# Tables of a diagonal state space built in slices during an expert layer, norms on 128 columns, and a fused bias and maximum in two attentions

## What is computed

```
def rmsnorm(x, w):
    y = xf * lax.rsqrt(jnp.mean(xf * xf, axis=-1, keepdims=True) + EPS)
    return (y * w.astype(jnp.float32)).astype(x.dtype)

# first block, layer: h = modulate(rmsnorm(x, norm1_w), shift1, scale1); mixer; x = x + gate1 * mix
#                     h2 = modulate(rmsnorm(x, norm2_w), shift2, scale2); x = x + gate2 * hier_moe(h2)
# chunk_attention:
scores = jnp.einsum('bclhd,bcshd->bchls', q, k_band) * (ATT_HEAD_DIM ** -0.5)
scores = scores + bias[None, None]
p = jax.nn.softmax(scores, axis=-1)

# second block: rms_norm; gmlp and fox_attention; later s5_mixer, feed-forward, gate
# fox_attention (q and k normalised, c the running sum of the log gates):
s = jnp.einsum('bqhd,bkhd->bhqk', qi, k) * scale
s = s + ci.transpose(0, 2, 1)[..., None] - ck[:, :, None, :]
s = jnp.where(kpos[None, :] <= pi[:, None], s, NEG_INF)

# s5_mixer, from a_re, a_im, log_dt, b_re, b_im alone, so from weights:
mag = jnp.exp(lr * dt)
ab_re, ab_im = mag * jnp.cos(li * dt), mag * jnp.sin(li * dt)
bb_re = cr[..., None] * br - ci[..., None] * bi
bb_im = cr[..., None] * bi + ci[..., None] * br
```

## Time and profile before

| what | value |
|---|---|
| median of 3 runs | 2632.39 us (2631.26 to 2634.85) |
| the profiled execution | 2631.74 us, span 2630.0 us |
| mean granted TensorE clock of that execution | 0.944 of full speed |
| PE busy | 2366.2 us (90%) |
| DVE busy | 1558.4 us (59%) |
| ACT busy | 700.7 us (27%) |
| POOL busy | 1484.7 us (56%) |
| DMA | 374.40 MB, 142 GB/s on average |

### The profile page before, as it was taken

One profiled execution on the slowest core, in us unless ns is written; L12 is line 12 of the kernel. 1 busy time (PEld: TensorE's weight loads), 2 busy tenths in 40 slices (PEclk: granted clock), 3 DMA queues, 4 the chain that ended last, 5 costly groups with the idle time before them and its releaser, 6 DMA issues.

```text
span 2630.0 us, 33090 instructions
## 1 busy us (share of the span) xinstructions
PE 2366.2 (90%) x12200; PEld 1806.6 (69%) x12200; DVE 1558.4 (59%) x1986; ACT 700.7 (27%) x1170; POOL 1484.7 (56%) x1272
## 2 busy tenths in 40 slices
PE   4988989959999998896798799999987899999998
PEld 2764755537777776553585588888866788888887
DVE  6879832166878765224897666662249926666223
ACT  2113212223434422122223232220025613222011
POOL 4830345455554552553672166667779657666774
PEclk7977989979999997998897999999998999999999
DMA  8845879533323234994331133332330223333231
GB/s 318 255 162 206 293 285 360 190 125 105 102 91 112 93 112 178 393 357 163 84 116 60 49 96 96 96 96 93 114 97 25 57 64 96 96 96 96 88 112 64
DMA packets 316737, 374.40 MB, mean 142 GB/s; under 512 B 52250, under 2 KB 259886, under 8 KB 316502
## 3 DMA queue, kind: packets, MB, share of 16 engines
q1 hardware_dynamic: 253840, 313.82, 35.6%
q0 software_dynamic: 28352, 31.04, 3.6%
q10 hardware_dynamic: 34438, 28.08, 3.5%
HBM read 410.20 MB, written 39.68 MB: 171 GB/s over the span
## 4 chain that ended last, share of the span: by engine, by line
PE 29%; issue 24%; POOL 23%; DVE 11%; DMA 10%; ACT 1%; POOLq 0%; ACTq 0%; SPq 0%; DVEq 0%
POOL WL L853 15%; PE PAIR L545 6%; POOL WH L849 6%; PE PAIR L546 6%; PE PAIR L547 6%; DMA XG<-htok_scratch,GATHER_I 4%; PE BANK L1823 4%; DMA ADA_A<-in_ada_w 2%; PE BANK L2259 1%; PE PAIR L1847 1%; PE PAIR L1809 1%; DVE ADA_SUM L652 1%; DMA PAIR_W<-y_scratch 1%; POOL EXTRA_W L2007 1%; DMA RAW<-in_ffn_w_up 1%
## 5 line engine op out<-in xcount | busy, mean ns | idle before, releaser
L853 POOL TENSOR_TENSOR WL<-RAW,WH 128x512 fp32r<-128x512 f32 x584 | 819.0, 1432 | 12.2
L545 PE MATMUL PAIR<-HH,WH 128*128 128x512 f32 x1792 | 710.0, 396 | 39.4 <-POOL HL L1142 27.2
L546 PE MATMUL PAIR<-HL,WH 128*128 128x512 f32 x1792 | 700.9, 391 | 0.0
L547 PE MATMUL PAIR<-HH,WL 128*128 128x512 f32 x1792 | 700.7, 391 | 0.0
L848 POOL TENSOR_TENSOR TURN<-ONES 128x1 f32<-128x1 f32 x146 | 36.8, 252 | 848.7 <-PE PAIR L547 751.3
L545 PEld LDWEIGHTS PAIR<-HH,WH 128*128 128x128 f32 x1792 | 338.6, 189 | 123.2 <-issue 44.2
L546 PEld LDWEIGHTS PAIR<-HL,WH 128*128 128x128 f32 x1792 | 338.9, 189 | 71.0 <-issue 2.2
L547 PEld LDWEIGHTS PAIR<-HH,WL 128*128 128x128 f32 x1792 | 338.4, 189 | 71.5
L849 POOL TENSOR_SCALAR WH<-RAW 128x2048 fp32r<-128x2048 f32 x146 | 284.7, 1950 | 0.0
L545 PE MATMUL PAIR<-FHH,WH 128*128 128x512 f32 x352 | 138.7, 394 | 0.0
L547 PE MATMUL PAIR<-FHH,WL 128*128 128x512 f32 x352 | 138.0, 392 | 0.0
(11 more groups left out here) (540 smaller groups left out, 4074.7 us busy)
## 6 DMA issues: line engine op xcount, KB each, us to landing
PAIR_W<-in_moe_w SPq DMA_DIRECT2D x96, 1024.0 KB, 9.9
RAW<-in_ffn_w_up SPq DMA_DIRECT2D x88, 512.0 KB, 4.8
ADA_B<-in_ada_w SPq DMA_DIRECT2D x30, 1024.0 KB, 5.3
RAW<-in_ssm_w_in SPq DMA_DIRECT2D x48, 512.0 KB, 4.8
ADA_A<-in_ada_w SPq DMA_DIRECT2D x18, 1024.0 KB, 6.9
RAW<-in_ffn_w_down SPq DMA_DIRECT2D x32, 512.0 KB, 4.2
RAW<-in_ev_w_in SPq DMA_DIRECT2D x20, 512.0 KB, 4.6
RAW<-in_mix_w_in SPq DMA_DIRECT2D x16, 512.0 KB, 6.6
```

The lines of the kernel that those rows point to most:

```text
L545: nc.tensor.matmul(o, wh, xh, start=start, stop=False)
L546: nc.tensor.matmul(o, wh, xl, start=False, stop=False)
L547: return nc.tensor.matmul(o, wl, xh, start=False, stop=stop)
L853: ins = pool.tensor_tensor(WL[:, s, c], RAW[:, s, c], WH[:, s, c].bitcast(F32), ALU.subtract)
```

## The change

It has three parts.

1. *S5 tables.* All of the S5 table work (vectors, ratios, powers, BB, the angles, the eight turnings) leaves `dve_evin` and attention 1. It is cut into 19 pieces, `dve_s5_slice`, each run on DVE after `hidden(s)` of a step of `moe(1)`. ACT gets `act_s5_slice`: an Exp and the two BRAW loads at step 0, the sines at 2, saving BB at 8, the table sine at 11, and the eight savings of turning at 13 to 20 (formerly on SP's queue). TAB stays in SBUF, so its way through DRAM goes. `pe_s5_vectors` and POOL's index constants run before the experts.
2. *Norms 0, 2, 4 and 8 on 128 columns.* `pe_sums` uses four matmuls of 128 tokens with 32 columns of ONES, each into another group of 32 partitions. Root and reciprocal then run on 128x128. `pe_factor` spreads the result to a 128x512 bank with four matmuls, and the scaling reads that bank in PSUM. For FINAL the weighted sum is made by PE with the squared gains as weights.
3. *Attentions.* L1408 and L1413 become one `tensor_tensor_reduce`; the factor HD**-0.5 goes to the copy of Q0, to QK_GAIN and to MINUS_HEAD.

The core of the diff:

```
     def pe_norm(pe, n):
...
-            ins = nc.tensor.matmul(bank[:], ONES[:], SQ[:, k % 2, :], start=k == 0, stop=k == KD - 1)
+            ins = pe_sums(bank, 0, ONES[:, 0:32], SQ[:, k % 2, :], k == 0, k == KD - 1)
...
+    def pe_sums(bank, at, weights, tile, first, last):
+        for j in range(NT):
+            ins = nc.tensor.matmul(bank[32 * j:32 * j + 32, at:at + P], weights, tile[:, j * P:j * P + P], start=first, stop=last)
+        return ins
...
+    def pe_factor(b, at):
+        for j in range(NT):
+            ins = nc.tensor.matmul(BANK[b % 4][:, j * P:j * P + P], IDENT[:, 32 * j:32 * j + 1].broadcast_to([P, P]),
+                                   RSTD[:, at:at + P], start=True, stop=True)
+        ins.then_inc(bank_ready, 1)
...
     def act_norm_final(act):
...
-            act.e.activation(TMP[:, k % 2, :], X[:, k, :], ACT.Square, scale=norm_gain[FINAL](k)).then_inc(part_ready, 1)
...
     def dve_root(dve, n):
-        dve.e.tensor_scalar(RSTD[:], bank[:], 1.0 / D, EPS, ALU.mult, ALU.add).then_inc(var_ready, 1)
+        dve.e.tensor_scalar(tile, bank[:, 0:columns], 1.0 / D, EPS, ALU.mult, ALU.add).then_inc(var_ready, 1)
         dve.wait(root_ready)
-        dve.e.reciprocal(RSTD[:], RSTD[:]).then_inc(bank_free[b % 4], 1)
+        dve.e.reciprocal(tile, tile).then_inc(bank_free[b % 4], 1)
...
-                    ins = dve.e.scalar_tensor_tensor(s[:, h % 2, SEG[j]:SEG[j] + wide], bank[:, at:at + wide],
-                                                     HD ** -0.5, bias(h)[:, SEQ - wide:SEQ], ALU.mult, ALU.add)
+                    ins = dve.e.tensor_tensor_reduce(s[:, h % 2, SEG[j]:SEG[j] + wide], bank[:, at:at + wide],
+                                                     bias(h)[:, SEQ - wide:SEQ], 1.0, LOWEST, ALU.add, ALU.max,
+                                                     MX[:, h % 2, 0, j:j + 1])
...
-            for j in range(NT):
-                ins = dve.e.tensor_reduce(MX[:, h % 2, 0, j:j + 1], s[:, h % 2, SEG[j]:SEG[j] + P * (j + 1)], AX.X, ALU.max)
-            dve.link(ins)
...
-            elif h:
-                dve_s5_turning(dve, h - 1)
...
         for s in range(PAIRS):
             if s + 1 < PAIRS:
                 rows(s + 1)
             hidden(s)
+            if layer:
+                dve_s5_slice(dve, s)
...
+    def act_s5_slice(act, s):
+        if s == 0:
+            act_s5_exp(act)
+            act_s5_load_b(act)
+        if s == 2:
+            act_s5_vectors(act)
+        if s == 8:
+            act_s5_save_b(act)
+        if s == 11:
+            act_s5_tables(act)
+        if 13 <= s < 13 + KD:
+            act_s5_save_turning(act, s - 13)
...
+    def dve_s5_slice(dve, s):
+        if s == 1:
+            dve_s5_angles(dve)
+        if s == 2:
+            dve_s5_series(dve)
+        if s == 3:
+            dve_s5_first_power(dve)
+        if s == 4:
+            dve_s5_ratios(dve)
+        if s == 5:
+            dve_s5_powers(dve)
+        if s == 6:
+            dve_s5_step(dve)
+        if s == 7:
+            dve_s5_b(dve)
+        if s in (8, 9, 10):
+            dve_s5_turns(dve, s - 8)
+        if 12 <= s < 12 + KD:
+            dve_s5_turning(dve, s - 12)
...
-        sp_s5_reload(engine)
-        for i in range(2, 4):
-            load_unit(sp, *block_unit(w, i * 256))
-        sp_s5_save(engine)
```

More of the change, by code:

```diff
@@ L102, in make_plan @@
     plan.step("columns_rest", banks=5)
+    plan.step("factor0", banks=1)
     plan.step("mixin", units=8, pairs=8)
@@ L342, in build @@
     PAIR_W0 = sb("PAIR_W0", [P, 3, 2, D], F32, r)
+    r2 = region()
+    BRAW = sb("BRAW", [P, 2, S5_TILES, S5_C], F32, r2)
+    BB_PR = sb("BB_PR", [P, 4, S5_TILES, S5_C], F32, r2)
+    BB_NEW = sb("BB_NEW", [P, 2, S5_TILES, S5_C], F32, r2)
+    r2.close()
+    r2 = region()
+    TAB = sb("TAB", [P, 2, S5_TILES, S5_IDX], F32, r2)
+    r3 = region()
+    ANGLE = sb("ANGLE", [P, 2, S5_TILES, S5_IDX], F32, r3)
+    r3.close()
+    TURN_PR = sb("TURN_PR", [P, 4, S5_N], F32, r2)
+    TURN_NEW = sb("TURN_NEW", [P, 2, 2, 4, S5_N], F32, r2)
+    r2.close()
     HTOK = sb("HTOK", [P, NT, D], F32, r)
@@ L456, in build @@
     r = region()
[L457 to L475, removed]
+    VEC_GAP = sb("VEC_GAP", [P, 79104 // 4], F32, r)
     VEC = sb("VEC", [P, 23, S5_TILES], F32, r)
@@ L1132, in act_norm @@
         act.wait(sq_used)
[L1133 to L1136, removed]
+        act_root(act, RSTD[:, 0:P], var_ready)
+        act_high(act, n)
     def pool_norm(pool):
@@ L1174, in scale @@
                 dve.wait(h_ready)
[L1175 to L1178, removed]
+            dve.e.tensor_tensor(norm_buffer(k), X[:, k, :], factor[:], ALU.mult)\
+                 .then_inc(dve.chain if k < KD - 1 else bank_free[b % 4], 1)
         scale(0)
@@ L1220, in pe_mixin, with act_copy_pairs @@
             pe_ada(pe, q)
-    def act_copy_pairs(act, name, first, n, to, tokens, func=ACT.Copy):
+    def act_copy_pairs(act, name, first, n, to, tokens, func=ACT.Copy, scale=1.0):
         for i in range(n):
@@ L1948, in dve_moe @@
             dve_minus_head(dve)
-            dve_s5_angles(dve)
+            dve_final_gains(dve)
+            for par in range(2):
+                dve.e.wait_ge(turn_saved[par], 8 * KD)
         for tt in range(NT):
@@ L2994, in build @@
     GRID = 16384.0
-    def sp_s5_reload(engine):
-        w, sp = s5_sems, engine.e
-        engine.wait(w["spilled"], 32)
-        engine.wait(half_ready, 4)
-        sp.dma_start(TAB[:].rearrange("p a t n -> p (a t n)"), tab_dram).then_inc(w["tab_back"], 16)
-    def sp_s5_save(engine):
-        w, sp = s5_sems, engine.e
-        for k in range(KD):
-            par = k % 2
-            engine.wait(w["turning"], 2)
-            sp.dma_start(turn_dram[k], TURN_NEW[:, par].rearrange("p a t n -> p (a t n)")).then_inc(turn_saved[par], 16)
-        for par in range(2):
-            engine.wait(turn_saved[par], 8 * KD)
     def sp_s5_tables(engine, first, last):
@@ L3016, in sp_s5_tables @@
         if first == 0:
+            engine.wait(w["spilled"], 16)
+            for par in range(2):
+                engine.wait(turn_saved[par], 8 * KD)
             sp.dma_start(BB[:].rearrange("p a t c -> p (a t c)"), bb_dram).then_inc(w["reloaded"], 16)
@@ L3526, in dve_s5_start, with dve_s5_turns @@
         dve.wait(w["bb"])
-        dve.wait(w["index"])
+    def dve_s5_turns(dve, part):
+        w = s5_sems
         x, n = ANGLE[:, 0], ANGLE[:, 1]
```

247 lines of the change are left out of this document (150 added, 97 removed).

## The result

The changed kernel takes 2597.34 us (median of 4 runs, 2595.06 to 2598.33), the kernel before 2633.3 us in the same runs. The ratio is 0.9863, 95% interval 0.9846 to 0.988. The prediction was 2594, from 2573 to 2615. The profiled execution has a span of 2596.5 us against 2630.0.

What follows compares the result with a forecast made beforehand. Bounds differ by stretch: PE in evin, DVE in attentions and S5 loop, DMA in layer two's experts, short chains in norms. Terms -26 -7 -3 -1 -9 -4 +12 = -38 gave 2594 us, own range 2582 to 2606, wider 2573 to 2615.

Steps and rivals of the forecast that it cites:

- Norm 2: Norm ahead of HL: smaller reciprocal and sums free over 4 us, but POOL's second weight block limits the gain to 3.
- Final norm: DVE's weighted sums go to PE; factor stands at about 1253, POOL's second block is late next; gain 9 us.
- Evin: Layer two's input matrices: some 60 us of DVE work leave, but PE is full, so 0 us.
- Attention 0: Fused instruction saves 1.66 per head; 1.2 taken for six of eight heads, PE close behind; gain 7 us.
- Norm 8: Norm before the S5 loop: cheaper sums, reciprocal and HF, partly given back by waiting for PE and longer DVE work; gain 4.
- attention 1: DVE falls to 3.7 per head, PE late next at 6.5 to 7; with the first output pair, gain 26 us.
- Rival (c): Attentions: fused instruction costs both old ones; attention 0 gains nothing, attention 1 stays PE-bound; 2601 us, chance 0.14.
- the experts: Layer two's experts: moved S5 work costs 12 us, near its 16 of DMA time, with ACT's 4 inside.
- Rival (b): Layer two's experts: BRAW loads block ACT and gathers behind full queues, costing 27 us; 2609 us, chance 0.17.
- DMA term for the savings: Layer two's experts: five of eight savings of turning fall before 1175 at 1.3 us each, 6.5 in all.
- DVE hides the slices: Layer two's experts: 60 us of slices on 19 steps delay nothing while a step stays within 7.0 us.
- Rival (d): Layer two's experts: slices don't fit, or the DVE port holds POOL's gathers, up to 2 us a step; slower, chance 0.05.

Runs made afterwards that it cites:

- tables_only: The kernel before with the S5 tables moved and nothing else; 2641.83 us, ratio 1.0017 against the kernel before.
- norms_only: The kernel before with the norms' part of the change alone; 2615.03 us, ratio 0.9926 against the kernel before.
- b_in_evin: The changed kernel with B's loads, product BB and its saving put back into the evin stage; 2587.94 us, ratio 0.9817 against the kernel before.
- saves_small: b_in_evin with the eight savings of turning cut to a sixteenth of their bytes; 2576.16 us, ratio 0.9795 against the kernel before.
- b_by_sp: The changed kernel with B's two loads issued by SP behind its first nine weight loads; 2590.15 us, ratio 0.9835 against the kernel before.

## Why the prediction came out right

**Right, with its reason.** Norm 2: POOL is late, and the gain (2.7 for 3) is that of POOL's end. Final norm (10.9 for 9): POOL's block ends 0.28 ahead of HL, but the factor, which was to be there some 4 us before it, comes with it, and ACT's HH ends the wait. Evin, with PE full, takes the same time without the DVE work that left it (132.1 for 132.6). Attention 0 (6.6 for 7, and 7.3 on average over all kernels) is right in its number; which engine is late there was not tested. Norm 8 gave 4.6 up to the first state step, and of this 1.9 is lost in the S5 loop, to 2.7 (forecast 4). Of the two things that the forecast said would give back, the wait for PE is there (1.60 at the first state step, 1.46 in the loop); longer work of DVE beside POOL is not, as its busy time is the same. PE's clock behind the loop takes 1.6 more, which the forecast did not have.

**Right in sum, with a wrong reason: attention 1.** Predicted was 26, measured 23.6 (20.9 in attention 1 for 24, 2.7 in the first pair for 2). The prediction said that PE is late next at 6.5 to 7 because its busy sum is above DVE's 3.7, and that a fused instruction of double length would leave this as it is. Heads do take 6.52. But tables_only shows that with the old two instructions DVE's sum of 5.6, also under 6.5, gives 8.18. The step that failed is taking the larger busy sum for what comes next; the wait that takes over is the loop through both queues, and that it came to 6.51, level with PE, is luck. Rival (c), priced at 2601, would by that have been worth 1.67 more on each head. The gain of 2.9 was also counted for seven heads. The first of them gave nothing: PE turned the second head 11.95 us after the first in the kernel before and 12.49 after it in the changed one, at half clock in both. And the 2 us of the first pair came as forecast, but norms_only has them without the change.

**Mis-sized: the experts, +16.6 for +12.** The two terms were there. ACT held by the issue was put at 5.14, the row of evin, and measured 15.09; it alone stopped PE for 11.27. An ACT stall over 8 us at step 0 was one of the prediction's own signs of being wrong, and it came. Rival (b) said this for ACT, but priced it at +27. The DMA term for the savings (five of the eight ahead of the last weight load) was 6.5; in b_in_evin all eight cost 12.6 by the traces and about 6 by the ratios. One wait for a gather behind them took 5.36 us and left half clock behind it (5.72 for 3.67). The "DVE hides the slices" step is right (204.2 in saves_small), though its margin was 0.9 and not 2.9.

The whole came out within 3.3 us of the forecast partly since errors of both signs met. Against the table, the stages are 9.0 us slower than forecast in five places (4.6 of it the experts, 2.4 attention 1) and 4.5 faster in four (1.9 of it the final norm).

**Rival (c), the fused instruction that costs both.** The Trainium skill, "VectorE: DVE Perf Modes", section "Two Vector instructions with no wait between them", counts an operation that writes its accumulator as two. The trace agrees, and gives the second its size: 0.08. The rival is out.

**Rival (d), the port.** POOL's issues in layer two's experts show an effect beside the slices: 96 of them took 100.4 us in all for 96.6, and eleven took over 1.15 us, the longest 1.76, where one had before. A DVE instruction was running when ten of the eleven began, nine of them of a slice. By the Trainium skill, "SBUF — State Buffer", section "SBUF: two separate sides", a DMA issued by GpSimd is held up while VectorE holds the port that the two share. The trace agrees in kind. The price here is 3.8 us of POOL's time in the whole stage and not 2 a step, and in saves_small the experts are as fast as without any DVE slice (204.2 for 205.6).

## What to carry to other kernels

Where two engines hand work to each other within a head, write down the loop (who waits for whom, and what stands ahead of it in the same queue) and add up its latency. The longest of that sum and the busy sums of the engines says what a head takes, and an edit gives only what it takes off the longest, down to the next one. Work moved under another stage has to be priced by the queue it is issued from and by how full the DMA engines are there, as an issue that took 5 us in one place took 15 in the other. Work moved between two steps fits only if it and the engine's own work together are under the step's period.

## What was not expected of the hardware

- A DMA of 4096 pieces of 64 bytes takes 0.46 us to issue when it is the first. The next one held its engine: ACT for 5.14 us in evin and for 15.09 in the experts, where the DMA engines are full; SP for 2.96 in b_by_sp. ACT was free about 1 us before the first of the two had landed (16.6 us after its issue). The same bytes in 128 pieces took 0.46.
- Saving 512 KB in the full stretch took 5.1 to 8.8 us from issue to landing, against 2.6 to 3.1 in attention 1.
- A scaling that reads its factor from PSUM ran at 0.67 us beside POOL's work (5.36 for eight in norm 8), where the one from SBUF took 1.17.
